# Attention-head gate loaded in two halves, and the products of the gate row placed on other units

## What is computed

```python
mod = silu(c) @ w_ada + b_ada                 # last third: the gate row
y_mla = attention(q, k, v) * silu(gate_mla)   # 8 heads, width 128 each
y_ret = retention(...) * silu(gate_ret)       # 4 heads, width 512 each
merged = sigmoid(merge_mla) * (y_mla @ w_proj_mla) \
       + sigmoid(merge_ret) * (y_ret @ w_proj_ret)
x = x + gate * (merged @ w_out)
return rmsnorm(x, g_final)
```

## Time and profile before

| what | value |
|---|---|
| median of 3 runs | 1579.26 us (1577.84 to 1579.91) |
| the profiled execution, its time | 1582.74 us |
| its span, first to last instruction | 1580.9 us |
| PE busy | 1541.4 us |
| DVE busy | 970.1 us |
| ACT busy | 668.3 us |
| POOL busy | 458.4 us |
| mean granted TensorE clock | 0.994 of full speed |

### The profile page before, as it was taken

The page is one execution under the profiler, slowest core; times in us unless marked ns, Lnnn a source line. Parts: engine busy times, 40 slices in busy tenths (PEclk is TensorE's granted clock), DMA queues, the critical chain, the costliest instruction groups (busy, mean ns, idle before and its releaser), DMA issues.

```text
span 1580.9 us, 20493 instructions
## 1 busy us (share of the span) xinstructions
PE 1541.4 (97%) x7472; PEld 1289.0 (82%) x7472; DVE 970.1 (61%) x1591; ACT 668.3 (42%) x1144; POOL 458.4 (29%) x388
## 2 busy tenths in 40 slices
PE   5999999999999999999999999999999999999998
PEld 4788888888888888788888888888778888878886
DVE  6884444444444448752566676666776776789644
ACT  7553355543333353342343343435554444445311
POOL 0032223332222200200344444454643343423000
PEclk9999999999999999999999999999999999999999
DMA  9343233332333334699577676657977777888432
GB/s 382 98 136 113 110 111 111 109 113 107 112 122 113 94 102 140 253 413 345 181 243 243 229 256 227 238 196 252 325 248 255 241 240 239 309 283 294 152 107 80
DMA packets 157316, 313.20 MB, mean 198 GB/s; under 512 B 12816, under 2 KB 87696, under 8 KB 148512
## 3 DMA queue, kind: packets, MB, share of 16 engines
q1 hardware_dynamic: 140384, 279.44, 50.7%
q0 software_dynamic: 4640, 16.84, 3.0%
q10 hardware_dynamic: 12192, 15.60, 3.0%
HBM read 201.47 MB, written 109.31 MB: 197 GB/s over the span
## 4 chain that ended last, share of the span: by engine, by line
PE 83%; DVE 5%; DMA 5%; issue 2%; ACT 2%; POOL 2%; ACTq 0%; SPq 0%; POOLq 0%; DVEq 0%
PE p_banks L2492 10%; PE p_banks L2452 10%; PE p_banks L2453 10%; PE p_banks L2450 10%; PE p_banks L2524 5%; PE p_banks L2365 2%; PE p_banks L2367 2%; PE p_banks L2366 2%; PE p_banks L2734 2%; PE p_banks L2602 2%; PE p_banks L2736 2%; PE p_banks L2764 2%; PE p_banks L2763 2%; PE p_banks L2737 2%; PE p_banks L2765 2%
## 5 line engine op out<-in xcount | busy, mean ns | idle before, releaser
L1923 DVE TENSOR_TENSOR w_form<-w_pair,w_form 128x512 fp32r<-128x512 f32 x150 | 116.2, 776 | 124.9 <-ACT w_form L1496 123.3
L1496 ACT ACTIVATE w_form<-w_pair 128x512 fp32r<-128x512 f32 x150 | 94.7, 632 | 217.1 <-PE p_banks L2453 211.7
L1578 ACT ACTIVATE prob<-p_banks,neg_max 128x128 f32<-128x128 f32 (+3 forms) x64 | 47.5, 742 | 187.4 <-DVE neg_max L2050 187.4
L2450 PE MATMUL p_banks<-h_hi,w_form 128*128 128x512 f32 x300 | 116.7, 389 | 0.0
L2452 PE MATMUL p_banks<-h_lo,w_form 128*128 128x512 f32 x300 | 116.7, 389 | 0.0
L2453 PE MATMUL p_banks<-h_hi,w_form 128*128 128x512 f32 x300 | 116.7, 389 | 0.0
L1219 POOL TENSOR_TENSOR w_pair<-w_pair 128x512 f32<-128x512 f32 x25 | 32.5, 1299 | 235.4 <-DVE w_form L1923 235.4
L2734 PE MATMUL p_banks<-t_hi,w_hi 128*128 128x512 f32 x224 | 88.2, 394 | 2.7 <-DVE t_lo L1691 2.7
L619 DVE TENSOR_TENSOR w_lo<-w_raw,w_hi 128x1024 fp32r<-128x1024 f32 (+3 forms) x63 | 69.8, 1110 | 30.2 <-ACT w_hi L598 29.6
L2736 PE MATMUL p_banks<-t_lo,w_hi 128*128 128x512 f32 x224 | 87.9, 392 | 0.0
L1305 POOL TENSOR_TENSOR qk_by_sine<-rotation_raw,rotation_table 128x512 f32<-128x512 f32 x32 | 41.9, 1310 | 158.4 <-DMA rotation_raw<-qk_chunks 110.9
(11 more groups left out here) (346 smaller groups left out, 4472.7 us busy)
## 6 DMA issues: line engine op xcount, KB each, us to landing
w_pair<-in_w_pairs SPq DMA_DIRECT2D x25, 1024.0 KB, 4.9
v_ret<-v_stage POOLq DMA_DIRECT2D x32, 512.0 KB, 5.7
v_chunk<-v_ret SPq DMA_DIRECT2D x32, 512.0 KB, 3.7
w_raw<-in_w_ret SPq DMA_DIRECT2D x28, 512.0 KB, 5.1
w_raw<-in_w_dense SPq DMA_DIRECT2D x23, 512.0 KB, 6.0
act_t<-stage SPq DMA_DIRECT2D x40, 256.0 KB, 2.0
act_t<-stage_late SPq DMA_DIRECT2D x40, 256.0 KB, 2.0
ada<-in_w_ada SPq DMA_DIRECT2D x4, 2048.0 KB, 24.8
```

The lines of the kernel that those rows point to most:

```text
L1496: self.nc.scalar.activation(self.form[f % FORM_SLOTS][:, 0, :], self.form_source(f), ACT.Copy).then_inc(self.form_hi, 1)
L1923: nc.vector.tensor_tensor(self.form[f % FORM_SLOTS][:, 1, :], self.form_source(f), self.form[f % FORM_SLOTS][:, 0, :].bitcast(F32), ALU.su ...
L2450: self.nc.tensor.matmul(out, w_hi[:, cut], x_hi[:, q, :], start=fresh and q == 0, stop=False, skip_group_check=True)
```

## The change

The gate of a head is loaded in two halves of 512 tokens. Half 0 is loaded behind the store of the second quarter of the head before, half 1 behind the store of its last quarter. DVE waits for half 0 before the first quarter and for half 1 before the third. Each half has its own semaphore, so the count from which the merge's second tiles start goes from 64 to 128. In the merge, product 5 of the gate row goes from unit 9 to unit 11, product 6 from unit 10 to unit 11, product 7 from unit 11 to unit 12, and the split of the row from unit 12 to unit 13. SP's iterations and its waits are as they were.

```diff
-YR_FROM, SECOND_FROM = 16, 64
+YR_FROM, SECOND_FROM = 16, 128
-GATE_ROW_AT, GATE_ROW_UNIT = 4, 24
+GATE_ROW, GATE_ROW_DONE, GATE_ROW_UNIT = {4: (0,), 5: (1,), 6: (2,), 7: (3,), 8: (4,), 11: (5, 6), 12: (7,)}, 13, 24
@@ sync
-        self.load_head_gate(sp, 0)
+        self.load_head_gate(sp, 0, 0)
+        self.load_head_gate(sp, 0, 1)
@@
-    def load_head_gate(self, sp, h):
+    def load_head_gate(self, sp, h, half):
         if h:
-            sp.wait_ge(self.y_done, 4 * h)
-        sp.dma_start(self.head_gate[:, :], self.d["act_t"][h]).then_inc(self.head_gate_loaded[h % 2], 16)
+            sp.wait_ge(self.y_done, 4 * h - 2 + 2 * half)
+        cut = slice(half * HALF, (half + 1) * HALF)
+        sp.dma_start(self.head_gate[:, cut], self.d["act_t"][h][:, cut]).then_inc(self.head_gate_loaded[half], 16)
@@ sync_attention
-                if q == NT // 2 - 1 and head < H_MLA - 1:
-                    self.load_head_gate(sp, head + 1)
+                if q % 2 and head < H_MLA - 1:
+                    self.load_head_gate(sp, head + 1, q // 2)
@@ scalar_output
-            if u == GATE_ROW_AT + KD:
+            if u == GATE_ROW_DONE:
@@ vector_attention
-                if q == 0:
-                    dve.wait_ge(self.head_gate_loaded[h % 2], 16 * (h // 2 + 1))
+                if q % 2 == 0:
+                    dve.wait_ge(self.head_gate_loaded[q // 2], 16 * (h + 1))
@@ vector_output
-            if 0 <= u - GATE_ROW_AT < KD:
-                self.weigh_gate(dve, u - GATE_ROW_AT)
-            elif u == GATE_ROW_AT + KD:
+            for k in GATE_ROW.get(u, ()):
+                self.weigh_gate(dve, k)
+            if u == GATE_ROW_DONE:
```

## The result

| | before | after |
|---|---|---|
| median device time | 1579.15 us (1577.84 to 1579.91, 4 runs) | 1590.16 us (1586.72 to 1594.88, 4 runs) |
| the profiled execution, its time | 1582.74 us | 1594.88 us |
| its span | 1580.9 us | 1593.1 us |

The change makes the kernel slower: the ratio is 1.0073, with a 95% interval from 1.0046 to 1.0099. Both profiled executions took longer than usual: that of before is above all four of its runs, that of after is the slowest of its four, 4.7 us above the median. Lines of the changed kernel are two higher than before behind the head gate's load: L2734 is now L2736.

A forecast was written before the change was run, and what follows sets the result against it. PE, busy 1541.4 us, bounds the kernel, so only its pauses and clock can be won. Terms -1.56 (halves), +2.1 (merge), +0.8 (clock falls), +0.7 (landing) sum to +2.0 us: 1581.3 us, range 1576.5 to 1585.0.

The forecast's parts named there:

- The pause at 937: PE's pause behind DVE's late head gate load: PE wins its whole 0.40 us.
- that at 1016: PE's pause behind DVE's second gate wait: v_stage's lowering starts 1.16 us earlier, pause shrinks from 1.45 to 0.29.
- SP's wait in iteration 10: Merge: gate row 7 waits for product 5, now later, so tile 15 is issued 6.6 us later.
- the extra issues: Head gate halves: eight more SP issues, about 0.43 us each, delay only the rotation's transfers; costed at nothing.
- My bound of 3.4: Cost in us of the eight more SP issues if POOL's low load gave no cover.
- -1.56: Head gate halves: total gain in us from PE's two shorter pauses, at 937 and 1016.
- The queue is empty by then, so I take 0: Merge gates 2 and 3 behind SP's second gate-row wait: lateness of 0 to 2.5 us, taken as 0.
- The pause at unit 20: Merge, group 3 for unit 20: operand ready at 1448.5, 1.8 us behind PE.
- these 2.5 us go, since it is late: DVE in the merge, 1408.03 to 1446.0: its idle 0.93 and 1.57 us at ends of units vanish.
- the gain of 1.5 us from the clock: Merge unit 12: PE's pause before group 3 falls from 2.11 to 1.24 us, so the clock stays at 1.00.
- the clock is not won: Rival: PE's clock did not fall in unprofiled runs, so before loses 1.5 less; +3.5 us, 1582.8; chance 0.12.
- The slower rival: SP's gate-row wait fully stalls the merge at tile 15, landing 6 us or more; +5.0 us, 1584.3; chance 0.22.

The follow-up runs named there:

- e13_sp_two: Kernel before, products in place, SP's iteration 10 wait lengthened to product 6 and its iteration 13 wait to the row's low part: ratio 1.0040.
- e17_tile18_first: e2_row with SP's second gate-row wait and the two merge gates behind it moved to iteration 14, behind tile 18's load: ratio 1.0032 against the kernel before.
- e2_row: Kernel before with only the gate row's products moved, the gate of a head loaded whole: ratio 1.0046 against the kernel before.
- e8_after_again: The whole change unaltered, measured again beside its parts on one chip: ratio 1.0043 against the kernel before.
- e12_row_ten: e2_row with product 5 in unit 10 instead of unit 11, product 6 in unit 11: ratio 1.0040 against the kernel before.
- e3_row_sp: e2_row with SP loading row 7 of the gate's weights in iteration 12, behind the operand loads, instead of iteration 10: ratio 1.0016 against the kernel before.

## Why the prediction was wrong

**Right.** DVE's waits for the gate go. The pause at 937 goes with them, and that at 1016 shrinks to 0.20 (0.29 predicted). SP's wait in iteration 10 holds tile 15 and what stands behind it; row 7 was issued 70.4 us behind the merge's first pause instead of 64.8, 5.5 us later for my 6.6, and PE paused at the predicted places: 0.25 and 0.19 for tiles 15 and 16 (predicted 0.5 and 0.6), 1.50 at unit 16 (1.8), and unit 20.

**Wrong, first: the extra issues. I wrote "what stands behind them is the rotation's transfers, which feed POOL, busy 29% of the span", and "I cost them at nothing".** POOL's load is no cover for a serial chain. The chain of load, turn, store takes 325 of attention's 346 us in the kernel before, 32 steps of 10.2 us in the mean, so it has little slack, and its last store stands in SP's order ahead of retention's first loads. Measured: 3.6 us in retention after, 3.5 between the means of the four such kernels and the eleven with the whole gate. My bound of 3.4, from the issues' own time, had the size by chance and not the mechanism. In time the halves came out at nothing (1.0000) where I had -1.56; the interval reaches from -1.7 to +1.9 us, so time alone doesn't refute that number, the traces refute its reason.

**Wrong, second: "The queue is empty by then, so I take 0".** I priced the late merge gates behind SP's second wait and waved off tiles 18 and 19 ("wanted some two units later"). They are issued 8 us late against the merge's start (1421.91 less 1336.31, before 1409.27 less 1331.80), and ACT and DVE wait for them or for the operand behind them. The pause at unit 20 was predicted at 1.8, in a chain where "these 2.5 us go, since it is late"; the idle times went, but new ones of 0.75, 0.25, 1.96 and 0.51 us came. DVE finished the last lowering 5.0 us later than before where I had 2.5, and PE was there 1.1 us earlier than I had it. The lowering's own 3.36 us were in my chain, as 3.42. The pause measured 5.15 (3.68 to 5.22 in the like kernels), and the clock behind it cost 3.1 us where I had 0.8 for all falls. e13_sp_two has the same stop with no product moved, only SP's two waits lengthened; e17_tile18_first got back only a part by loading tile 18 ahead of the wait, so the rest of the row's cost is not assigned.

**Wrong, third: the gain of 1.5 us from the clock.** Nine more traces of this stretch with the row and its products in place have pauses of 1.27 to 1.77 us ahead of unit 12, and behind all nine the clock is 1.00. The 2.11 us with its fall belonged to the one execution that I read. The merge takes 130.7 us in the mean of eight traces with the row and SP's waits as before, that of before among them, not 132.3; against that the moved row costs 8.3 us (139.0 in three traces). This is the rival "the clock is not won". The Trainium skill (TensorE: Matmul & The Clock Gate, "What's actually happening") says that the same kernel can lose a different number of matmuls to the clock from run to run. The traces agree that the loss differs, but not with the page's reason, a monitor that runs free of the program: in them the pause itself differed, from 1.27 to 2.11 us, and the clock went with its length.

The slower rival had the right kind of end, a full stop of the merge with the clock falling, but put it at tile 15 and a landing of 6 us or more. Tile 15 was there 4.6 us behind its issue. The stop came at tile 18 and unit 20, and tile 18 did land slowly: ACT began its split 7.4 us behind the issue in after, and 6.2 to 7.2 in the like kernels (e2_row, e8_after_again, e12_row_ten, e13_sp_two).

## What to carry to other kernels

An engine that issues transfers in a fixed order turns each wait into a wait for all that stands behind it. When work is moved later, list every wait on its result, not only the first, and follow the longest-delayed load through to its consumers. A chain of small transfers that feeds an idle engine can still be the tightest chain of a stretch: compare its steps times their length with the stretch, not its engine's busy share. A mend that puts one load ahead of a wait puts another behind it, so read the trace of the mended kernel for new waits. And a term that rests on one pause of one execution needs a second trace, or a wide bound.

## What the runs showed of the hardware

A fall of PE's clock went with the pause's length in every place that was read. In the merge, behind pauses of 1.87, 2.11, 2.56, 2.94, 3.07 and 3.68 to 5.22 us (ten in all) the granted clock of the next 4.0 us was 0.50 to 0.64, that is mostly the level of 1.2 GHz. Behind the twenty-four pauses of 0.68 to 1.77 us it was 1.00.

DVE's lowerings of 128x1024 took up to 3.43 us instead of 1.22 when they met a subtraction of POOL (3.42 in the kernel before, 3.36 in after, 3.39 in e3_row_sp); the 2.2 us more are about one such subtraction (2.39). So a transfer that lands earlier can lengthen a step on the path, as in e3_row_sp, where POOL's third subtraction made a lowering 2.2 us longer on the path.
